# The sub-norm of block 1 in two parts, its first tile turned inside the attention

## The reference

```
a  = diff_attention(dq, dk, dv, lam, pos)                 # 4 heads of 128
a  = a * rsqrt(mean(a*a, -1) + 1e-5) * g_subln * (1 - lambda_init)
bo = dsa_attention(...)                                   # 4 heads of 64, top-k keys
co = forgetting_attention(...)                            # 4 heads of 64
mixed = concatenate([a, bo, co]) * silu(gate)
out = mixed @ w_out
x = layer_norm(ALPHA * x + out, ln_g, ln_b)
```

## Time and profile before

| what | us |
|---|---|
| median of 3 runs | 2950.2 (2950.14 to 2951.24) |
| the profiled execution | 2955.67 |
| its span, first to last instruction | 2953.9 |
| TensorE matmuls busy | 2807.7 |
| VectorE busy | 1143.5 |
| ScalarE busy | 758.1 |
| TensorE, wait for the first gated tile, each layer | 5.2 |

### The profile page before, as it was taken

One profiled execution on the slowest core, in us unless ns is written; L12 is line 12 of the kernel. 1 busy time (PEld: TensorE's weight loads), 2 busy tenths in 40 slices (PEclk: granted clock), 3 DMA queues, 4 the chain that ended last, 5 costly groups with the idle time before them and its releaser, 6 DMA issues. The chain is left out here.

```text
span 2953.9 us, 65188 instructions
## 1 busy us (share of the span) xinstructions
PE 2807.7 (95%) x27105; PEld 1660.8 (56%) x27109; DVE 1143.5 (39%) x2779; ACT 758.1 (26%) x1596; POOL 324.0 (11%) x584
## 2 busy tenths in 40 slices
PE   8999999999889999999999999989899999999996
PEld 4444655444554457645666666644675566666663
DVE  2572653472654335545211122263453511222114
ACT  1111531110542147611111111143674111111111
POOL 3000430000440000011010000020000100000101
PEclk9999999999989999999999999999999999999998
DMA  7112653211753100046999999962002699999994
GB/s 272 69 57 81 235 161 97 76 68 57 239 184 136 57 1 2 34 189 225 396 401 401 397 401 400 391 234 95 1 2 108 227 385 397 401 400 402 400 401 144
DMA packets 155504, 636.94 MB, mean 216 GB/s; under 512 B 19744, under 2 KB 24352, under 8 KB 138960
## 3 DMA queue, kind: packets, MB, share of 16 engines
q1 hardware_dynamic: 114624, 517.59, 45.4%
q0 software_dynamic: 40720, 117.18, 11.6%
HBM read 582.70 MB, written 52.00 MB: 215 GB/s over the span
## 5 line engine op out<-in xcount | busy, mean ns | idle before, releaser
L1108 PE MATMUL PJ<-WR,XT 128*128 128x512 f32 (+2 forms) x1152 | 477.3, 570 | 4.9 <-ACT XT L140 2.4
L140 ACT ACTIVATE PT<-TR 128x512 f32<-128x512 f32 (+3 forms) x384 | 177.8, 493 | 884.4 <-PE TR L1337 730.5
L1108 PEld LDWEIGHTS PJ<-WR,XT 128*128 128x128 f32 x1152 | 216.5, 192 | 244.2 <-issue 216.9
L140 DVE TENSOR_TENSOR PR<-G 128x384 f32<-128x384 f32 x64 | 35.7, 559 | 736.2 <-ACT G L140 735.8
L1066 PE MATMUL PJ<-WR,XT 128*128 128x512 f32 x576 | 260.1, 608 | 1.5 <-ACT XT L140 1.4
L1317 PE MATMUL SC<-QK,XT 128*64 128x256 f32 x2112 | 242.0, 382 | 0.0
L140 DVE TENSOR_REDUCE SM<-SC 128x1 f32<-128x768 f32 (+6 forms) x208 | 173.7, 835 | 161.1 <-PE SC L1086 153.1
L1268 PE MATMUL PJ<-WR,XT 128*128 128x512 f32 x512 | 225.6, 592 | 1.0 <-issue 1.0
L1317 PE MATMUL SC<-WR,XT 128*64 128x256 f32 x1984 | 226.2, 381 | 0.0
L140 ACT ACTIVATE PR<-SC,SM 128x256 f32<-128x256 f32 (+5 forms) x288 | 187.6, 669 | 36.9 <-DVE SM L140 26.0
L1317 PEld LDWEIGHTS SC<-QK,XT 128*64 128x64 f32 x2112 | 149.2, 137 | 84.9 <-issue 13.9
(11 more groups left out here) (251 smaller groups left out, 3345.3 us busy)
## 6 DMA issues: line engine op xcount, KB each, us to landing
QK<-in_w_gate_dram SPq DMA_DIRECT2D x34, 2048.0 KB, 9.6
WR<-in_w_down_dram SPq DMA_DIRECT2D x34, 2048.0 KB, 15.8
QK<-in_w_up_dram SPq DMA_DIRECT2D x32, 2048.0 KB, 13.3
WR<-in_w_up_dram SPq DMA_DIRECT2D x32, 2048.0 KB, 14.5
WR<-in_w_gate_dram SPq DMA_DIRECT2D x30, 2048.0 KB, 9.5
QK<-in_w_down_dram SPq DMA_DIRECT2D x30, 2048.0 KB, 16.0
WR<-in_w_ada_dram SPq DMA_DIRECT2D x24, 2048.0 KB, 8.1
WR<-in_w_in_dram SPq DMA_DIRECT2D x14, 2048.0 KB, 7.9
```

Of the source, the lines that this page charges most:

```text
L140: return lambda *a, **k: Signal(make(*a, **k), self)
L1108: m = mm(bank[:, 0:n], XT1[:, c, s.t * P:(s.t + 1) * P], w[:, c, 0:n], start=c == 0, stop=c == DC - 1)
```

## The change

The sub-norm becomes two steps. Part 0 stands at the end of iteration 28 of the attention: it takes the root of the twelve sums of tiles 0 to 2 and scales and gates tile 0. At the end of iteration 30 tile 0 is turned. Part 1 stands where the sub-norm stood: it scales and gates tile 1 (with the root that it has), takes the root of tile 3's four sums, and then scales and gates tiles 2 and 3.

```
-        attend(unit_list, extra={i: ada(j) for j, i in enumerate(ADA_AT)})
-        add("subln", l=l)
+        turned = {}
+
+        def mixturn(t, l=l):
+            turned[t] = add("mix_turn", t=t, l=l, tr=take("tr", 2)).tr[-1]
+
+        def first_mixed(l=l):
+            add("subln", l=l, part=0, front=(), roots=(0, 3), tiles=(0,))
+
+        extra = {i: ada(j) for j, i in enumerate(ADA_AT)}
+        extra[28] = first_mixed
+        extra[30] = lambda: mixturn(0)
+        attend(unit_list, extra=extra)
+        add("subln", l=l, part=1, front=(1,), roots=(3, 4), tiles=(2, 3))
...
-        turned = {}
-
-        def mixturn(t, l=l):
-            turned[t] = add("mix_turn", t=t, l=l, tr=take("tr", 2)).tr[-1]
-
-        mixturn(0)
...
-                    act.wait_ge(sub_in, s.l + 1)
-                    A(RS, SS, ACT.Sqrt).then_inc(sub_out, 1)
+                    act.wait_ge(sub_in, 2 * s.l + s.part + 1)
+                    roots = slice(4 * s.roots[0], 4 * s.roots[1])
+                    A(RS[:, roots], SS[:, roots], ACT.Sqrt).then_inc(sub_out, 1)
...
+                    def normed_heads(tiles):
+                        for t in tiles:
+                            for h in range(4):
+                                a = ARAW[:, (4 * t + h) * P:(4 * t + h + 1) * P]
+                                x = STT(a, a, RS[:, 4 * t + h:4 * t + h + 1], GSUB, ALU.mult, ALU.mult)
+                            now(x)
+                            TT(G1[:, t, 0:512], G1[:, t, 0:512], ARAW[:, 512 * t:512 * t + 512], ALU.mult).then_inc(sub_done, 1)
+
+                    normed_heads(s.front)
+                    roots = slice(4 * s.roots[0], 4 * s.roots[1])
+                    dve.wait_ge(square_done, 16 * s.l + 4 * s.roots[1])
+                    now(TS(SS[:, roots], SS[:, roots], 1.0 / P, EPS1, ALU.mult, ALU.add))
                     v.increment(dve, sub_in, 1)
-                    dve.wait_ge(sub_out, s.l + 1)
-                    now(reciprocal(RS, RS))
-                    now(TS(RS, RS, 1.0 - lam_init, None, ALU.mult))
+                    dve.wait_ge(sub_out, 2 * s.l + s.part + 1)
+                    now(reciprocal(RS[:, roots], RS[:, roots]))
+                    now(TS(RS[:, roots], RS[:, roots], 1.0 - lam_init, None, ALU.mult))
+                    normed_heads(s.tiles)
```

More of the change, by code:

```diff
@@ L153, in __init__ @@
                  tr_before=None, src_tr=None, after=None, tiles=None, turns=None, slot=None, loads=None, prev=None,
-                 cols=None, half=None, base=None, order=None, xe0=None, keys=None, full=None, inner=None, near=None, moe=None):
+                 cols=None, half=None, base=None, order=None, xe0=None, keys=None, full=None, inner=None, near=None, moe=None,
+                 part=None, front=(), roots=None):
         self.kind, self.l, self.t, self.h, self.j, self.c, self.e = kind, l, t, h, j, c, e
@@ L168, in __init__ @@
         self.near, self.moe = near, moe
+        self.part, self.front, self.roots = part, front, roots
 def make_plan(until=99):
@@ L2061, in _ @@
                     lam_init = 0.8 - 0.6 * math.exp(-0.3 * s.l)
-                    dve.wait_ge(square_done, 16 * (s.l + 1))
-                    now(TS(SS, SS, 1.0 / P, EPS1, ALU.mult, ALU.add))
-                    v.increment(dve, sub_in, 1)
-                    dve.wait_ge(sub_out, s.l + 1)
-                    now(reciprocal(RS, RS))
-                    now(TS(RS, RS, 1.0 - lam_init, None, ALU.mult))
[L2068 to L2073, removed]
+                    def normed_heads(tiles):
[9 more added lines that the diff above has]
+                    now(TS(SS[:, roots], SS[:, roots], 1.0 / P, EPS1, ALU.mult, ALU.add))
+                    v.increment(dve, sub_in, 1)
+                    dve.wait_ge(sub_out, 2 * s.l + s.part + 1)
+                    now(reciprocal(RS[:, roots], RS[:, roots]))
+                    now(TS(RS[:, roots], RS[:, roots], 1.0 - lam_init, None, ALU.mult))
+                    normed_heads(s.tiles)
                 elif s.kind == "wout":
```

## The result

The kernel after took 2958.4 us, the kernel before 2950.2 (medians of 17 runs each on one chip); the ratio is 1.0028, interval 1.0021 to 1.0034. Two further comparisons gave 1.0034 (1.0020 to 1.0048) and 1.0025 (1.0016 to 1.0034). The forecast of 2955.1 was 3.3 too low. The median lies in the range and, by 0.1, in the forecast's own range, but the loss of 0.28% is just past the 0.2% at which I drew the line between "same" and "slower".

A forecast was written before the change was run, and what follows sets the result against it. TensorE, busy 95% of the span, bounds the kernel, so only its waits pay. Layer 0 -2.4 and layer 1 +7.3 give +4.9: 2955.7 becomes 2960.6, less 5.5 to the median, forecast 2955.1 us; range 2949.3 to 2960.3, own range 2952.2 to 2958.5.

The forecast's parts named there:

- The detour: VectorE, inside the attention: part 0's instructions and the wait for the root make unit 29's minimum start 4.95 us late.
- d: Lateness of the attention's end: at least 5.6 us, taken as 6.8.
- the clock's term: TensorE at 1.2 GHz from the wait before unit 28's turn to about 847, taking the lateness from 5.6 to 6.8 us.
- Layer 0's gain: Layer 0, attention's end to tile 1's first projection: 9.2 minus the lateness of the attention's end, 2.4 us gained.
- 414.6 + d: Layer 0: when tile 1's first projection can start: rows landing at 413.9, plus d, plus 0.7 for a vector product.
- Layer 1's loss: Layer 1: the chain from last ada through store, loads and context turns moves by d as a whole; 7.3 us lost.
- The 0.5 for the clock: Layer 1's second projection finds the clock down at its start: 0.5 us more, between 0 and 1.3.
- The upper bound for d: Lower clock lasting through unit 29's turn, next weighing and ada: 2.6 us more, d = 9, sum +10.1.
- That both layers pay: Rival: clock down for long, attention's end about 9 us late in both layers; +9.3, 2959.5 us; chance 0.15.
- That layer 1's chain doesn't move: Rival: DMA engines, not the ada, set layer 1's store; only layer 0 counts, -2.4, 2947.8 us; chance 0.11.
- That the detour is hidden: Rival: VectorE's slack swallows the added work, the attention's end is 1.0 late; -7.2, 2943.0 us; chance 0.08.
- That each table switch pays a drain: Rival: about 1.38 us of drain per ScalarE table switch, sum +7.7, 2957.9 us; chance 0.05.

The follow-up runs named there:

- the filled one: The changed kernel plus three constant matmuls filling TensorE's wait before unit 28's turn in both layers; ratio to before 1.0027, +8 us.
- layer 0 alone: Sub-norm split only in layer 0, layer 1 as in the kernel before; measured twice: ratios to before 1.0015 and 1.0010, +4.4 and +3.0 us.
- after a third time: The changed kernel unaltered, measured again in the third batch; ratio to before 1.0025, +7.4 us.
- the turn behind: The changed kernel with tile 0 turned after the attention as before, part 0 still inside it, both layers; ratio to before 1.0032.
- the detour out of the way: The changed kernel with sums formed at iteration 28, tile 0 gated at the end of 29 and turned at 32; ratio to before 0.9988, -3.5 us.
- both repairs: The changed kernel with sums, gating and turn spread over iterations 28 to 32 and row loads issued first; 2938.6 us, ratio to before 0.9962.

## Why the prediction was right in kind and short in size

- **The detour: right.** Forecast 4.95 on VectorE, measured 5.03; a wait "of about 3 us" before unit 28's turn, measured 2.98 and 3.09; unit 29's turn 5.5 late, measured 5.8 and 5.9; and d at least 5.6, where the last ada came 5.84 late in layer 0. The second table load, costed at nothing, cost nothing: ScalarE still waits 1.06 before unit 30's exponential.
- **d: too high by the clock's term.** Forecast 6.8, measured 5.8 in layer 0 in every trace, and 6.0 to 7.0 in layer 1 (mean 6.4). The term that was mis-sized is the 1.2 for the clock. I had it low for some 7 us. In layer 0 it came in every trace but the filled one (tile 0's turn took 1.58 to 1.97, in the filled one 1.13), but in the first trace it was back after about 3 us (granted 0.64 over 392.4 to 394, 0.50 over 394 to 396, 0.95 over 396 to 398.5), and the ada was 5.8 late with it and without: ScalarE's copies covered it. In layer 1 it came in three of five, and the ada was 7.0 late only in the two in which it lasted over the scores (1.59 instead of 1.13).
- **Layer 0's gain: the term that was mis-sized most.** Forecast 2.4, measured 0.7 on average, between +2.8 and -2.4. A lower d gave 1.0 back. The step "414.6 + d" took the store's time and the landing of 6.4 from one execution, at the short end of both, and put tile 1's projection 22.4 behind the last ada; it came 24.0 behind it on average, 1.6 later. The wait before it, forecast "under 2 us", was that in two of six traces. And the wait, now 2.6 long, cost the clock: 1.0 more in the projection behind it. 2.4 + 1.0 - 1.6 - 1.0 = 0.8, the 0.7 but for rounding.
- **Layer 1's loss: right in kind, forecast 7.3, measured 6.4 (5.8 against the two traces of before alone).** The chain moves as a whole; from the last ada to the second projection it took 33.0 on average over five traces and 32.9 over two of before. What moves is d, 6.4, where I had 6.8. The 0.5 for the clock isn't there: the second projection took 15.3 on average (14.5 to 16.1). In before's two traces it took 16.0, but in the two of layer 0 alone, whose layer 1 is as before, 14.4; over these four it is 15.2. The change doesn't move it.
- **The sum: +4.9 forecast, +5.1 to +5.8 by the two blocks, +7.4 to +10.0 by the times.** That the blocks come so near the forecast is luck: a gain 1.7 too high and a loss 0.9 to 1.5 too high cancel. And the times show more. Of the twelve measurements of variants eleven lie 1.7 to 8.0 us above the blocks of their trace, those that gain included (-11.2 against -13.5, -3.5 against -5.2), layer 0 alone most (+4.4 against -3.6), and one 0.7 below (after a third time). A single trace need not stand for the median, but the sign is nearly always the same. One lead is the stretch between the blocks, from layer 1's first projection to its last but one ada. In the four traces that leave layer 0's attention as it was it took 363.2 to 363.5. In the seven that have layer 0 as in after it took 361.9 to 366.8, on average 1.4 more; in the other three (the turn behind, the detour out of the way, both repairs) 362.2 to 363.4. The change does nothing in this stretch, and no run tests why it should differ. A part of the loss, 2 to 3 us of the 8.2, stays open.
- **The sums themselves.** The upper bound for d adds 2.6 to 6.8, which is 9.4 and not 9; the sum with it is +10.9 instead of +10.1. No trace came near it.
- **The class.** "Same" at 0.57 rested on a line of 5.9 us and a forecast one below it. With the unplaced 2 to 3 us the result fell on the far side, and by the same 2 to 3 us it kept inside its own range by only 0.1.
- **The rivals.** That both layers pay, the lower clock long in both: its mechanism is refuted, as d was never above 7.0 and the filled wait changed nothing. Its outcome, that layer 0 loses too, isn't: by the blocks layer 0 gains 0.6 to 0.7 on average, by the times of layer 0 alone it loses 3.0 to 4.4. That layer 1's chain doesn't move: refuted, it moved by d. That the detour is hidden: refuted as built, but it is what the unblocked version makes true: d fell to 0.3, below the 4.3 named, and the time fell below before's. That each table switch pays a drain: refuted by 831.71, where load, root and hand-over take 1.54 behind a busy ScalarE, as in the earlier trace rows; by the rule of the Trainium skill (ScalarE: Activation LUTs, section What ACT_TABLE_LOAD costs) the reciprocal would stand 1.4 later.

## What to carry to other kernels

A stage that waits for two things gains from a faster first one only by the distance to the second, and that distance should be taken from several executions, as the second was a DMA chain whose parts varied by over 1 us each. Before moving work into a region where every engine hands over to the next, ask whose queue it stands in: the same eight instructions on VectorE and the tile's turn made the last ada 5.8 us late at one place, where a table load had to be waited for, and 0.3 at another, the root already taken and the turn behind the last ada. Of the 5.8, 3.2 were the eight instructions' and 2.6 the turn's. And small constants that are broadcast to all partitions are large loads: put the rows that someone waits for ahead of them.

## What was not expected of the hardware

The same wait of 3.09 us on TensorE, in layer 1, left the granted clock at 2.4 GHz in one execution of the kernel and brought 1.2 GHz in another (the turn behind it 0.66 and 1.11, tile 0's 1.09 and 1.97). A cost of the clock behind a short wait is thus an average, here up to 1.0 us in layer 1 and 0 to 2.5 in the projection behind layer 0's wait (7.10 and 9.60 behind 1.64 and 4.21). There too waits of almost the same length went both ways: 7.11 behind 2.94, granted clock 1.00, and 8.64 behind 2.97, granted clock 0.50 at first.
